# Tile 0 first in the last three pieces of a stage, a reordered norm, and GpSimd making three low parts

## The chip, the core and the metric

The kernel runs on one core of a Trainium2 chip. The metric is the device time of one execution in microseconds (us), the median of several runs. The engines are TensorE (PE, its weight loads are PEld), VectorE (DVE), ScalarE (ACT), GpSimd (POOL) and SyncE (SP), which here only issues weight transfers.

## The reference, cut to what matters

Two layers act on 256 rows of 1024 float32 values. Each layer has two sub-layers, and each sub-layer ends in a residual and two normalizations:

```python
shift, scale, gate = ada_modulation(c, w_mod_mix[layer], b_mod_mix[layer])
h = normalize(x) * (1.0 + scale) + shift
mix = token_mixer(h, pos, w_in[layer], ...)
x = layer_norm(DEEPNORM_ALPHA * x + (1.0 + gate) * mix, ln_mix_g[layer], ln_mix_b[layer])
shift, scale, gate = ada_modulation(c, w_mod_ffn[layer], b_mod_ffn[layer])
h = normalize(x) * (1.0 + scale) + shift
ff = swiglu(h, ...)          # layer 0; moe_swiglu(h, ...) with top 2 of 8 experts in layer 1
x = layer_norm(DEEPNORM_ALPHA * x + (1.0 + gate) * ff, ln_ffn_g[layer], ln_ffn_b[layer])
```

`token_mixer` is three branches (two kinds of attention and a pooling mixer), gated and merged, and ends in `merged @ w_out`. `swiglu` is `(silu(h @ w1) * (h @ w3)) @ w2`.

## The kernel before

**Pieces.** All weights stream through the core in pieces of 1 MB (128 x 2048 values). SyncE loads a piece into one of six slots of `w_raw`. ScalarE rounds it into `w_hi` (three slots; L467, in the experts L711), and VectorE makes the remainder `w_lo = w_raw - w_hi` (L830, L1219). A float32 product is then three matmuls: hi x hi, hi x lo and lo x hi (L1344 to L1346). Activations are split in the same way, into `actT_hi` (ScalarE, L501) and `actT_lo` (VectorE, L916). Pieces called "mod" carry the weights of the next sub-layer's shift, scale and gate. VectorE alone works on those (L855) and adds them up in `mod_acc`.

**Semaphores.** `split_hi` counts rounded pieces. `piece_used` counts pieces whose `w_raw` slot is free again, which is when `w_lo` is there. `split_used` counts pieces whose `w_hi` and `w_lo` slots TensorE has finished with. ScalarE rounds piece j only after TensorE has finished piece j - 3. The order of work on every engine is written out by hand; there is no planner.

**Tiles and stages.** The 256 rows are two tiles of 128. A piece is used on tile 0 and then on tile 1, 12 matmuls each. The stages are: MIX of layer 0 (27 pieces for TensorE: in, gate, branch, out), DENSE (33 pieces), MIX of layer 1, and a loop over eight experts. In MIX, piece "out" (n, h) is column half n and row half h of `w_out`, in the order (0,0), (1,0), (0,1), (1,1). DENSE goes by panels: A and B are up-projections, C is the down-projection. The gated panel is turned (transposed) by TensorE and split into `gT_hi` and `gT_lo` (L654, L1116) before its C pieces. The last panel is half as wide, so the last three pieces are C (4,0), C (4,1) and C (5,0).

**The end of a stage.** The last two pieces run tile by tile: both on tile 0, which signals `out_sent` (or `y_sent`), then both on tile 1 (L1612 to L1621, L1688 to L1695). In DENSE the last panel is turned after C (4,0) has run on both tiles (L1699). Then `open_sublayer` (L1370) broadcasts shift and scale over all rows by matmuls with ones (L1367, 4 float32 matmuls in 8 passes), transposes tile 0 of the new h (L1362), and broadcasts gate (L1378). `second_tile` transposes tile 1 (its `gate1_ready` wait is for ScalarE's L495). The next stage's first three pieces run on tile 0, then on tile 1; `second_tile` stands after piece 1 on tile 0. At the start of the experts there are no such pieces: the router follows tile 1.

**The norm between stages** (`norms`, L919 for VectorE, L504 for ScalarE, called three times, for `sub` 1, 2 and 3). For tile t VectorE does: `residual` (L892, L895), `statistics` of it (L875, L878 to L880), `inverse_std` (L884, after ScalarE's square root L484), `layer_norm` (L900, L901), `statistics` of x, `inverse_std`, `modulate` (L906, L909), `rest_of_h` (L916). L906 needs 1 + scale, which ScalarE makes in place (L489) after L1367. The order on VectorE is: `ahead(0)`, tile 0 up to the statistics of x, `ahead(1)`, residual and statistics of tile 1, modulation of tile 0, layer norm of tile 1, `rest_of_h` of tile 0, statistics and modulation of tile 1, `ahead(2)`, `rest_of_h` of tile 1. `ahead(i)` is the rounding (ScalarE) or the low part (VectorE) of the next stage's piece i.

**GpSimd** clears `mod_acc` (L416), and its queue issues the transfers of biases, norm rows and small tables (L418 to L437). It clears `yacc` and `zeros` before the experts (L451, L452). It does no arithmetic on weights.

Of the kernel before, what the change touches and what calls it, by code (L numbers as in the profile page):

```python
# [23 lines left out]
F32 = mybir.dt.float32  # L24
# [6 lines left out]
P = 128  # L31
# [168 lines left out]
def trunk(nc, I, consts, out):  # L200
    with ExitStack() as ctx:
# [70 lines left out]

        ident = cst[:, C_IDENT:C_IDENT + P]
# [26 lines left out]
        x_ready = sem("x_ready")  # L300
# [112 lines left out]
        def _(gp):  # L413
# [9 lines left out]

            nc.gpsimd.memset(mod_acc[:, :], 0.0).then_inc(acc_zero, 1)
# [4 lines left out]
            for layer in range(DEPTH):  # L429
# [4 lines left out]
                for par in range(2):  # L434
# [8 lines left out]
                        I["ln_mix_b"][bass.ds(layer, 1), :].rearrange("a d -> (a d)"))  # L443
                if layer < 1:
# [3 lines left out]
                    ln_rows(I["ln_ffn_g"][0], I["ln_ffn_b"][0])  # L448
                else:
# [9 lines left out]
        def _(act):  # L459
# [44 lines left out]
            def norms(sub, n, free, held, ahead):  # L504


                ahead(0)
                root(n + 1, 0)
                ahead(1)
                root(n + 2, 0)  # L510
                one_plus_scale(sub, free)
                root(n + 3, 1)
                ahead(2)
                round_h(sub, 0, held)
                root(n + 4, 1)
                one_plus_gate(sub, held)
                round_h(sub, 1, held)
# [13 lines left out]
            for layer in range(DEPTH):  # L531
# [111 lines left out]
                def panel_events(stretch, panels, split_base, panel0, blocks):  # L643
# [6 lines left out]
                    def gT_part(p):  # L650
                        act.wait_ge(gT_sent, panel0 + p + 1)
                        w = panels[p]
                        for b in range(blocks):
                            ins = A(gT_hi[:, b, 0:w // P, :], ps[:, HW1 + 2 * b, 0:w].rearrange("p (c q) -> p c q", q=P), ACT.Copy)  # L654
# [168 lines left out]
        def _(dve):  # L823
# [95 lines left out]
            def norms(chain, sub, n, free, held, f, f_done, n_ln, ahead):  # L919
# [3 lines left out]
                ahead(0)  # L923
# [21 lines left out]
                ahead(2)  # L945
# [25 lines left out]
            for layer in range(DEPTH):  # L971
# [119 lines left out]
                def yT_rest(c):  # L1091
# [4 lines left out]
                layer_loads = [MIX.landed[s] + DENSE.landed[s] for s in range(RING)]  # L1096
                stream(MIX, [layer * layer_loads[s] + MOD0.landed[s] for s in range(RING)], sbase,
# [3 lines left out]
                      layer * 64 + 32,  # L1101
                      lambda i: rest_of_piece(DENSE, i, sbase + MIX.n_split))
                assert chain.n == DVE_MIX_STEPS, chain.n

                def panel_events(stretch, panels, split_base, panel0, blocks):
# [6 lines left out]
                    def gT_part(p):  # L1112
                        dve.wait_ge(gT_hi_ready, panel0 + p + 1)
                        w = panels[p]
                        for b in range(blocks):
                            ins = TTn(gT_lo[:, b, 0:w // P, :], ps[:, HW1 + 2 * b, 0:w].rearrange("p (c q) -> p c q", q=P),  # L1116
                                      gT_hi[:, b, 0:w // P, :].bitcast(F32), ALU.subtract)
# [19 lines left out]
                if layer < 1:  # L1137
                    chain = Chain(dve, dve_ffn, 0)
                    stream(DENSE, [MOD0.landed[s] + MIX.landed[s] for s in range(RING)], MIX.n_split,
                           MOD0.n + MIX.n, 6 * MODS, 2, panel_events(DENSE, DENSE_PANELS, MIX.n_split, 0, 2))  # L1140
                    norms(chain, 2, 6, 4, 0, lambda t, c: bank(2 * t + c),
                          lambda t: dve.wait_ge(split_used, LAYER_SPLITS + SPLIT) if t else dve.wait_ge(y_sent, 1), 64,
                          lambda i: rest_of_piece(MIX, i, LAYER_SPLITS))
                    assert chain.n == DVE_DENSE_STEPS, chain.n
                else:
# [63 lines left out]
                    dve.wait_ge(yacc_zero, 1)  # L1209
                    with nc.Fori(0, EXPERTS, engines=[dve.engine], hint_back_edge=True, head_slot={dve.engine: 0}) as e:  # L1210
# [128 lines left out]
        def _(pe):  # L1339
# [30 lines left out]
            def open_sublayer(sub, free, held, gate_pieces=None):  # L1370
# [25 lines left out]
            for layer in range(DEPTH):  # L1396
# [147 lines left out]
                for i in range(SPLIT):  # L1544
# [4 lines left out]
                    if i == 1:  # L1549
# [6 lines left out]
                for i, piece in enumerate(MIX.pieces):  # L1556
# [41 lines left out]
                    elif h == 0:  # L1598
                        if n == 0:
                            pe.wait_ge(mT_hi_ready, layer * 2 + 1)  # L1600
                            pe.wait_ge(mT_lo_ready, layer * 2 + 1)
                        if n == 0:
# [294 lines left out]
```

## Time and profile before

| | |
|---|---|
| median of 3 runs | 1860.01 us (1859.79 to 1860.46) |
| the profiled execution | 1864.31 us |
| its span, first to last instruction | 1861.5 us |
| TensorE busy | 1686.1 us (91% of the span) |
| VectorE busy | 1408.1 us (76%) |
| ScalarE busy | 1035.7 us (56%) |
| GpSimd busy | 26.1 us (1%) |
| mean DMA rate | 270 GB/s |

A share of busy time is a mean over all stages. The chain that ended last says which engine's work or wait set the end at each moment. A timeline row gives start, duration, engine, source line, operation, output and inputs with shapes, how many instructions are merged, and in brackets how long the engine had been idle before and what released it. Matmul durations overlap in the pipeline, so the rate is read from the distance between starts.

### The profile page before, as it was taken

The page shows a single profiled execution, that of the slowest core. Times are in us where ns is not written, and L with a number is a line of the kernel's source. Part 1 is how long each engine was busy: PE and PEld are TensorE (multiplying, and loading weights), DVE is VectorE, ACT ScalarE, POOL GpSimd, SP SyncE. Part 2 cuts the span into 40 slices and gives each one's busy share as a digit, 9 for nine tenths or more (in the row PEclk, how much of TensorE's full clock was granted, in tenths as well). Part 3 has the DMA queues.
Part 4 walks back from the last instruction along what each step waited for, and adds up shares of the span by engine and source line. Part 5 has one row for each costly group of instructions (what it writes and reads, how often), then busy time and mean ns, then how long its engine had stood idle before and what let it go on. Part 6 is the DMA issues. An engine that isn't in the chain of part 4 may idle for free.

```text
span 1861.5 us, 21366 instructions
## 1 busy us (share of the span) xinstructions
PE 1686.1 (91%) x7620; PEld 1340.1 (72%) x7621; DVE 1408.1 (76%) x1201; ACT 1035.7 (56%) x822; POOL 26.1 (1%) x32
## 2 busy tenths in 40 slices
PE   1899979998999857999999989999999899999995
PEld 0687758886787736777877768888677677887773
DVE  7785877676876874897888865556589688788887
ACT  1465334433465424777767745545477577776772
POOL 0100000000100000000000000000000000000000
PEclk9898989999998977999999989999999899999998
DMA  9874458765574352998998975676499799899992
GB/s 366 312 275 159 138 201 293 272 249 171 195 271 156 113 203 102 375 381 304 367 345 303 391 275 181 215 229 212 157 377 382 254 371 387 306 366 337 331 393 81
DMA packets 210539, 502.36 MB, mean 270 GB/s; under 512 B 9138, under 2 KB 13410, under 8 KB 210482
## 3 DMA queue, kind: packets, MB, share of 16 engines
q1 hardware_dynamic: 208770, 496.15, 74.4%
q0 software_dynamic: 1712, 5.43, 0.9%
q8 instruction: 39, 0.64, 0.2%
q14 instruction: 18, 0.14, 0.0%
HBM read 500.50 MB, written 1.05 MB: 269 GB/s over the span
## 4 chain that ended last, share of the span: by engine, by line
PE 78%; DVE 14%; issue 6%; ACT 1%; DMA 1%; POOL 0%; DVEq 0%; SPq 0%; ACTq 0%; POOLq 0%
PE ps L1344 21%; PE ps L1346 21%; PE ps L1345 21%; DVE w_lo L1219 4%; PE ps L1350 3%; PE ps L1351 3%; PE ps L1738 2%; PE ps L1851 2%; DVE mod_acc L855 1%; DVE w_lo L830 1%; PE ps L1776 1%; DVE stats L875 1%; PE ps L1468 1%; DVE gates L1024 1%; DVE hbuf L906 1%
## 5 line engine op out<-in xcount | busy, mean ns | idle before, releaser
L1219 DVE TENSOR_TENSOR w_lo<-w_raw,w_hi 128x2048 fp32r<-128x2048 f32 x333 | 757.7, 2289 | 228.0 <-ACT w_hi L711 225.7
L711 ACT CAST w_hi<-w_raw 128x2048 fp32r<-128x2048 f32 x333 | 634.5, 1910 | 254.5 <-PE ps L1346 165.0
L1344 PE MATMUL ps<-w_hi,actT_hi 128*128 128x512 f32 (+1 forms) x1536 | 613.7, 400 | 41.0 <-DVE w_lo L1219 16.6
L1346 PE MATMUL ps<-w_hi,actT_lo 128*128 128x512 f32 (+1 forms) x1536 | 598.4, 390 | 0.0
L1345 PE MATMUL ps<-w_lo,actT_hi 128*128 128x512 f32 (+1 forms) x1536 | 597.8, 389 | 0.0
L1344 PEld LDWEIGHTS ps<-w_hi,actT_hi 128*128 128x128 f32 x1536 | 292.8, 191 | 117.3 <-issue 29.6
L1346 PEld LDWEIGHTS ps<-w_hi,actT_lo 128*128 128x128 f32 x1536 | 292.3, 190 | 60.9
L1345 PEld LDWEIGHTS ps<-w_lo,actT_hi 128*128 128x128 f32 x1536 | 293.2, 191 | 57.0 <-issue 1.7
L830 DVE TENSOR_TENSOR w_lo<-w_raw,w_hi 128x2048 fp32r<-128x2048 f32 x90 | 205.8, 2289 | 120.7 <-ACT w_hi L467 120.5
L467 ACT CAST w_hi<-w_raw 128x2048 fp32r<-128x2048 f32 x90 | 171.2, 1909 | 132.9 <-PE ps L1346 124.7
L1350 PE MATMUL ps<-w_hi,gT_hi 128*128 128x512 f32 x336 | 141.7, 422 | 14.8 <-DVE gT_hi L1246 14.8
L1351 PE MATMUL ps<-w_lo,gT_hi 128*128 128x512 f32 x336 | 137.9, 410 | 0.0
L855 DVE SCALAR_TENSOR_TENSOR mod_acc<-w_raw,c_act,mod_acc 128x512 f32<-128x512 f32 x192 | 130.5, 746 | 0.4 <-DMA w_raw<-in_w_mod_mix_dram 0.4
L1344 PE MATMUL ps<-w_hi,gT_hi 128*128 128x512 f32 x256 | 104.2, 407 | 7.6 <-DVE gT_lo L1242 3.8
L1345 PE MATMUL ps<-w_lo,gT_hi 128*128 128x512 f32 x256 | 103.5, 404 | 0.0
L1346 PE MATMUL ps<-w_hi,gT_lo 128*128 128x512 f32 x256 | 102.8, 401 | 0.0
L1350 PEld LDWEIGHTS ps<-w_hi,gT_hi 128*128 128x128 f32 x336 | 66.3, 197 | 42.9 <-DVE w_lo L1219 28.3
L1351 PEld LDWEIGHTS ps<-w_lo,gT_hi 128*128 128x128 f32 x336 | 66.4, 198 | 14.9
L1344 PEld LDWEIGHTS ps<-w_hi,gT_hi 128*128 128x128 f32 x256 | 49.3, 193 | 23.1 <-issue 7.3
L1346 PEld LDWEIGHTS ps<-w_hi,gT_lo 128*128 128x128 f32 x256 | 49.3, 192 | 11.9
L1345 PEld LDWEIGHTS ps<-w_lo,gT_hi 128*128 128x128 f32 x256 | 49.2, 192 | 11.2
L721 ACT ACTIVATE silu<-ps 128x512 f32<-128x512 f32 x56 | 33.6, 599 | 39.2 <-PE ps L1346 38.9
(238 smaller groups left out, 1174.5 us busy)
## 6 DMA issues: line engine op xcount, KB each, us to landing
w_raw<-in_exp_w_dram SPq DMA_DIRECT2D x336, 1024.0 KB, 6.8
w_raw<-in_ffn_w_dram SPq DMA_DIRECT2D x33, 1024.0 KB, 5.2
w_raw<-in_w_mod_mix_dram SPq DMA_DIRECT2D x24, 1024.0 KB, 9.0
w_raw<-in_w_mod_ffn_dram SPq DMA_DIRECT2D x24, 1024.0 KB, 6.0
w_raw<-in_w_gate_dram SPq DMA_DIRECT2D x24, 1024.0 KB, 6.5
w_raw<-in_w_in_dram SPq DMA_DIRECT2D x14, 1024.0 KB, 7.1
w_raw<-in_w_out_dram SPq DMA_DIRECT2D x8, 1024.0 KB, 5.1
w_raw<-in_w_branch_c_dram SPq DMA_DIRECT2D x4, 1024.0 KB, 5.2
```

The lines of the kernel that those rows point to most:

```text
L467: nc.scalar.copy(w_hi[:, j % SPLIT, :], w_raw[:, i % RING, :]).then_inc(split_hi, 1)
L711: nc.scalar.copy(w_hi[:, i % SPLIT, :], w_raw[:, i % RING, :]).then_inc(split_hi, 1)
L830: TTn(w_lo[:, j % SPLIT, :], w_raw[:, i % RING, :], w_hi[:, j % SPLIT, :].bitcast(F32), ALU.subtract).then_inc(piece_used, 1)
L855: ins = STT(acc, w[:, k, n * BANK:(n + 1) * BANK], c_act[:, 2 * (q % 4) + k:2 * (q % 4) + k + 1], acc, ALU.mult, ALU.add)
L1219: TTn(w_lo[:, i % SPLIT, :], w_raw[:, i % RING, :], w_hi[:, i % SPLIT, :].bitcast(F32), ALU.subtract).then_inc(piece_used, 1)
L1344: MM(to, hi, w_h, start=first, stop=False)
L1345: MM(to, hi, w_l, start=False, stop=False)
L1346: return MM(to, lo, w_h, start=False, stop=last)
L1350: MM(to, packed, w_h, start=first, stop=False)
L1351: return MM(to, packed, w_l, start=False, stop=last)
L1738: ins = MM(to, part[:, t, k * P:(k + 1) * P], pick[:, t, b * P:(b + 1) * P], start=t == 0, stop=t == 1)
L1851: ins = MM(bank(2 * t + c), place[:, b, t * P:(t + 1) * P], hbuf[:, b, c * BANK:(c + 1) * BANK], start=b == 0, stop=b == blocks - 1)
```

## The change

VectorE no longer makes the low parts of the next stage's first three pieces at the three seams. GpSimd does, in `rest_of_first`. `ahead` is gone from VectorE's `norms`, and VectorE waits on `piece_used` for the three before its next stream. At a stage's end the last three pieces run on tile 0 and then on tile 1. In DENSE the last panel is turned after C (4,0) on tile 0 only, and the last panel's `gT` has its own place, in `h_lo`. The norm modulates tile 0 before it touches tile 1. The broadcast of gate (`send_gate`) stands on its own: it waits for `rows_read`, which VectorE sets after tile 1's residual has been read, and it comes after piece 0 on tile 0; `second_tile` comes after piece 2 on tile 0. The first MIX stage of layer 0 keeps its order.

```diff
+        gT_end_hi, gT_end_lo = (h_lo[:, part, 0:BANK].rearrange("p (b c q) -> p b c q", b=2, q=P) for part in range(2))
+        def gT_parts(p, panels):
+            return (gT_end_hi, gT_end_lo) if p == len(panels) - 1 else (gT_hi, gT_lo)
...
# GpSimd
+            def rest_of_first(split_base):
+
+                for i in range(SPLIT):
+                    gp.wait_ge(split_hi, split_base + i + 1)
+                    nc.gpsimd.tensor_tensor(w_lo[:, i, :], w_raw[:, i, :], w_hi[:, i, :].bitcast(F32),
+                                            ALU.subtract).then_inc(piece_used, 1)
...
                 ln_rows(I["ln_mix_g"][bass.ds(layer, 1), :].rearrange("a d -> (a d)"),
                         I["ln_mix_b"][bass.ds(layer, 1), :].rearrange("a d -> (a d)"))
+                rest_of_first(layer * LAYER_SPLITS + MIX.n_split)
                 if layer < 1:
                     gp.wait_ge(gate_sent, 2)
                     fresh_acc(I["b_mod_mix"][1:2, :], 2)
                     gp.wait_ge(x_ready, 2)
                     ln_rows(I["ln_ffn_g"][0], I["ln_ffn_b"][0])
+                    rest_of_first(LAYER_SPLITS)
...
# ScalarE, norms
+                root(n + 1, 0)
                 ahead(0)
-                root(n + 1, 0)
-                ahead(1)
                 root(n + 2, 0)
                 one_plus_scale(sub, free)
+                round_h(sub, 0, held)
+                ahead(1)
                 root(n + 3, 1)
                 ahead(2)
-                round_h(sub, 0, held)
+                one_plus_gate(sub, held)
                 root(n + 4, 1)
-                one_plus_gate(sub, held)
                 round_h(sub, 1, held)
...
# VectorE, norms
-                ahead(0)
                 dve.wait_ge(gate1_ready, sub)
                 f_done(0)
                 residual(chain, f, 0)
...
                 statistics(chain, x, 0)
-                ahead(1)
-                f_done(1)
-                residual(chain, f, 1)
-                statistics(chain, hbuf, 1)
                 inverse_std(chain, n + 2, 0)
                 dve.wait_ge(scale_ready, sub + 1)
                 modulate(chain, 0, free)
+                f_done(1)
+                residual(chain, f, 1)
+                dve.sem_inc(rows_read, 1)
+                rest_of_h(sub, 0, held)
+                statistics(chain, hbuf, 1)
                 inverse_std(chain, n + 3, 1)
                 chain.step(layer_norm(chain, 1))
-                rest_of_h(sub, 0, held)
                 statistics(chain, x, 1)
                 inverse_std(chain, n + 4, 1)
                 modulate(chain, 1, free)
-                ahead(2)
                 rest_of_h(sub, 1, held)
                 dve.sem_inc(x_ready, 1)
...
+                if layer:
+                    dve.wait_ge(piece_used, LAYER_PIECES + MOD0.n + SPLIT + RING)
...
+                    dve.wait_ge(piece_used, first_split)
...
# TensorE
+            def send_gate(sub, held):
+
+                if sub:
+                    pe.wait_ge(rows_read, sub)
                 for q in range(2):
                     ins = MM(bank(held + 2 + q), ones, mod_acc[:, (4 + q) * BANK:(5 + q) * BANK], start=True, stop=True)
                 ins.then_inc(gate_sent, 1)
...
-                    if i == 1:
+                    if layer and i == 0:
+                        send_gate(2, 0)
+                    if i == (2 if layer else 1):
                         second_tile(layer * 2, 0)
...
+                        merged_T(1)
+                    elif (n, h) == (1, 0):
+                        project_out(j, n, h, 0)
+                    else:
+
                         if n == 0:
+                            pe.wait_ge(mT_hi_ready, layer * 2 + 2)
+                            pe.wait_ge(mT_lo_ready, layer * 2 + 2)
+                        ins = project_out(j, n, h, 0)
+                        if n == 1:
+                            ins.then_inc(out_sent, 1)
+                            for m, (n, h) in enumerate([(1, 0), (0, 1), (1, 1)]):
+                                project_out(j - 2 + m, n, h, 1).then_inc(split_used, 1)
...
-                            if b == 0 and i == 1:
-                                second_tile(1, 4)
+                            if b == 0 and i == 0:
+                                send_gate(1, 4)
+                        if b == 0:
+                            second_tile(1, 4)
...
+                            if j >= stretch.n_split - SPLIT:
+                                ins = down(j, p, h, 0)
+                                if j == stretch.n_split - SPLIT:
+                                    turn(p + 1)
+                                if j == stretch.n_split - 1:
+                                    ins.then_inc(y_sent, 1)
+                                    for m, (_, p, h) in enumerate(stretch.pieces[-SPLIT:]):
+                                        down(j - SPLIT + 1 + m, p, h, 1).then_inc(split_used, 1)
                                 continue
...
                 else:
+                    send_gate(3, 4)
                     second_tile(3, 4)
```

## Rows read from the trace of the kernel before

**Rows 1.** The page, chain that ended last, shares of the span.

```profile
PE 78%; DVE 14%; issue 6%; ACT 1%; DMA 1%; POOL 0%; DVEq 0%; SPq 0%; ACTq 0%; POOLq 0%
```

**Rows 2.** Timeline, TensorE, 247 to 300: start us, us, engine, line, shapes, [idle before].

```profile
247.45 3.59 PE L1367 MATMUL ps<-mod_acc,cst 128*128 128x512 f32 x8
...
260.38 1.97 PE L1362 MATMUL ps<-cst,hbuf 128*128 128x128 f32 x8 [9.33 <-DVE hbuf L909]
...
270.44 1.03 PE L1362 MATMUL ps<-cst,hbuf 128*128 128x128 f32 x8
...
272.22 0.50 PE L1344 MATMUL ps<-w_hi,actT_hi 128*128 128x512 f32 x1 [0.75 <-DVE w_lo L830]
...
299.32 0.39 PE L1346 MATMUL ps<-w_hi,actT_lo 128*128 128x512 f32 x1
```

**Rows 3.** Timeline, TensorE, 444 to 481.

```profile
444.48 0.47 PE L1344 MATMUL ps<-w_hi,gT_hi 128*128 128x512 f32 x1 [1.63 <-DVE gT_lo L1116]
...
455.75 3.60 PE L1367 MATMUL ps<-mod_acc,cst 128*128 128x512 f32 x8
468.52 1.97 PE L1362 MATMUL ps<-cst,hbuf 128*128 128x128 f32 x8 [9.18 <-DVE hbuf L909]
...
480.37 0.50 PE L1344 MATMUL ps<-w_hi,actT_hi 128*128 128x512 f32 x1 [0.70 <-DVE w_lo L830]
```

**Rows 4.** Timeline, TensorE, 663 to 692.

```profile
663.80 3.59 PE L1367 MATMUL ps<-mod_acc,cst 128*128 128x512 f32 x8
680.59 1.97 PE L1362 MATMUL ps<-cst,hbuf 128*128 128x128 f32 x8 [13.19 <-DVE hbuf L909]
...
689.66 1.94 PE L1362 MATMUL ps<-cst,hbuf 128*128 128x128 f32 x8 [4.51 <-DVE hbuf L909]
```

**Rows 5.** Timeline, VectorE, 242 to 269.

```profile
242.28 1.29 DVE L892 TENSOR_TENSOR hbuf<-ps,gate 128x512 f32<-128x512 f32 x2 [1.33 <-PE ps L1346]
...
244.93 1.28 DVE L875 BATCH_NORM_STATS2 stats<-hbuf 128x6 f32<-128x512 f32 x2
...
247.19 1.29 DVE L900 SCALAR_TENSOR_TENSOR hbuf<-hbuf,mv,lnrow 128x1024 f32<-128x1024 f32 x1
248.51 1.28 DVE L901 SCALAR_TENSOR_TENSOR x_sb<-hbuf,rstd,lnrow 128x1024 f32<-128x1024 f32 x1
...
251.39 0.15 DVE L880 TENSOR_SCALAR veps<-mv 128x1 f32<-128x1 f32 x1
...
258.13 1.40 DVE L906 SCALAR_TENSOR_TENSOR hbuf<-x_sb,mv,ps 128x512 f32<-128x512 f32 x2
...
266.49 0.15 DVE L880 TENSOR_SCALAR veps<-mv 128x1 f32<-128x1 f32 x1
...
267.11 1.41 DVE L906 SCALAR_TENSOR_TENSOR hbuf<-x_sb,mv,ps 128x512 f32<-128x512 f32 x2
```

**Rows 6.** Timeline, VectorE, 662 to 694.

```profile
662.49 1.28 DVE L892 TENSOR_TENSOR hbuf<-ps,gate 128x512 f32<-128x512 f32 x2
...
692.30 1.28 DVE L916 TENSOR_TENSOR actT_lo<-ps,actT_hi 128x512 fp32r<-128x512 f32 x2
```

**Rows 7.** Timeline, ScalarE, 251 to 263.

```profile
251.69 1.06 ACT L489 ACTIVATE ps<-ps 128x512 f32<-128x512 f32 x2
...
258.17 1.88 ACT L467 CAST w_hi<-w_raw 128x2048 fp32r<-128x2048 f32 x1
...
262.38 0.60 ACT L501 ACTIVATE actT_hi<-ps 128x512 fp32r<-128x512 f32 x1 [0.25 <-PE ps L1362]
```

**Rows 8.** Timelines of GpSimd and VectorE, 478 to 482 and at 692.

```profile
478.03 2.28 DVE L830 TENSOR_TENSOR w_lo<-w_raw,w_hi 128x2048 fp32r<-128x2048 f32 x1
...
478.76 2.69 POOL L416 MEMSET mod_acc<- 128x3072 f32 x1
...
692.37 1.80 POOL L451 MEMSET yacc<- 128x2048 f32 x1 [47.79 <-DVEq L947]
```

**Rows 9.** Windows, TensorE: window, length, busy (count), granted clock, DMA share, GB/s.

```profile
254.00:257.00 3.00, 0.00 (x0) 0.52 0.73 177
```

More of the change, by code:

```diff
@@ L299, in trunk @@
         h_ready, hT_sent, hT_hi_ready, hT_lo_ready = sem("h_ready"), sem("hT_sent"), sem("hT_hi_ready"), sem("hT_lo_ready")
-        x_ready = sem("x_ready")
+        x_ready, rows_read = sem("x_ready"), sem("rows_read")
         dve_start, dve_mix, dve_ffn, act_mix = sem("dve_start"), sem("dve_mix"), sem("dve_ffn"), sem("act_mix")
@@ L917, in rest_of_h, with norms @@
                         ALU.subtract).then_inc(hT_lo_ready, 1)
-            def norms(chain, sub, n, free, held, f, f_done, n_ln, ahead):
-                ahead(0)
+            def norms(chain, sub, n, free, held, f, f_done, n_ln):
                 dve.wait_ge(gate1_ready, sub)
@@ L1115, in gT_part @@
                         for b in range(blocks):
-                            ins = TTn(gT_lo[:, b, 0:w // P, :], ps[:, HW1 + 2 * b, 0:w].rearrange("p (c q) -> p c q", q=P),
-                                      gT_hi[:, b, 0:w // P, :].bitcast(F32), ALU.subtract)
+                            hi, lo = (part[:, b, 0:w // P, :] for part in gT_parts(p, panels))
+                            ins = TTn(lo, ps[:, HW1 + 2 * b, 0:w].rearrange("p (c q) -> p c q", q=P), hi.bitcast(F32), ALU.subtract)
                         ins.then_inc(gT_lo_ready, 1)
@@ L1597, in _ @@
                         ins.then_inc(split_used, 1)
[L1598 to L1602, printed above, removed]
-                            pe.wait_ge(branch_read, layer * 6 + 4)
+                    elif (n, h) == (0, 0):
+                        pe.wait_ge(mT_hi_ready, layer * 2 + 1)
+                        pe.wait_ge(mT_lo_ready, layer * 2 + 1)
+                        pe.wait_ge(branch_read, layer * 6 + 4)
                         for t in range(TT):
@@ L1685, in swiglu @@
                                 pe.wait_ge(gT_lo_ready, panel0 + p + 1)
-                            if j == stretch.n_split - 2:
-                                continue
-                            if j == stretch.n_split - 1:
-                                for b in range(blocks):
-                                    ins = down(j - 1, p - 1, 1, b)
-                                    if b == blocks - 1:
-                                        ins.then_inc(split_used, 1)
-                                    ins = down(j, p, h, b)
-                                    ins.then_inc(split_used if b == blocks - 1 else y_sent, 1)
+                            if j >= stretch.n_split - SPLIT:
[6 more added lines that the diff above has]
+                                        down(j - SPLIT + 1 + m, p, h, 1).then_inc(split_used, 1)
                                 continue
```

28 lines of the change are left out of this document (9 added, 19 removed).

## The prediction

> **What bounds the kernel now.** I read first the page's chain that ended last: TensorE holds 78% of it and VectorE 14% [rows 1]. So time comes only from what TensorE waits for, and the change touches three places, the seams between stages, where it waits for VectorE. I call them seam 1 (attention part to dense part, layer 0), seam 2 (dense part to layer 1) and seam 3 (attention part to the experts). TensorE's timeline of each comes next. At seam 1 the eight passes that broadcast scale and shift (L1367) end at 251.04, then TensorE is idle 9.33 us until tile 0's transposes at 260.38, and the wait is for VectorE's L909 [rows 2]. Seam 2 has 9.18 us, and 1.63 us before it for the last gT_lo [rows 3]. Seam 3 has 13.19 us for tile 0 and 4.51 us for tile 1 [rows 4]. VectorE's timeline shows what it does meanwhile, a serial norm [rows 5]. I measure seams 1 and 2 by when TensorE starts tile 1 of the next stage's first three pieces. One piece on one tile is 12 matmuls; from 272.22 to 299.32 there are 119 steps, so 0.2277 us each and 2.73 us a piece [rows 2]. Piece 2 of tile 0 starts at 272.22 and 480.37; with 2.79 for its slower first step, tile 1 starts at 275.0 and 483.15 now.
>
> **Earlier start of tile 0's norm.** Three pieces instead of two are left for tile 1, so tile 0's sum is ready one piece, 2.73 us, sooner: VectorE's L892, now at 242.28, can start near 239.4. At seam 3 it now starts at 662.49, behind the w_lo subtraction that the norm issues first, ahead(0) [rows 6]; the last three pieces of tile 1 end at 663.80, so afterwards it starts at 663.80 - 3 x 2.73 = 655.6, 6.9 us sooner. Tile 1's pieces give their weight slots back later than now, which costs nothing: cast 0 goes behind the first square root, at 243.9 at seam 1, and GpSimd is through with piece 0 at about 251, before tile 0 needs it.
>
> **What is late next.** From L892 to the second L880 are 9.11 us, and L880 to L906 takes 0.62 when nothing is in between (266.49 to 267.11) [rows 5]: the norm of tile 0 could reach L906 9.73 after it starts, at 249.1, 455.4 and 665.3 (at seam 2 tile 0's sum will be ready at 445.7, which is 457.7 below less 3.6 for L1367 and 3 x 2.8 for tile 1's pieces). But L906 needs 1+scale, and that comes after all of tile 1's matmuls: L1367 ends at 251.04, 457.7 (459.35 less the 1.63 us wait, which goes because tile 0 of two other pieces covers the last turn) and 667.39 [rows 2 to 4]. ScalarE adds 1.06 us [rows 7] and two hand-overs make it 1.2. So L906 starts at M = 252.2, 458.9 and 668.6. Some 3 us of the earlier start are thus lost at each seam. Tile 0's transposes follow at M + 2.25 (258.13 to 260.38) [rows 2, 5].
>
> **After M, on VectorE:** modulation 2.89, residual of tile 1 2.65 (242.28 to 244.93), first half of L916 0.65 [rows 5, 6]. TensorE starts piece 0 at M + 6.25 and is done with it at M + 9; the two gate broadcasts (about 1.8 at full clock, 8 passes being 3.59) end at M + 10.8. VectorE goes on with the rest of L916 and the first statistics of tile 1 and reaches L900 at M + 9.25.
>
> **GpSimd.** ScalarE's second L501 ends 2.60 after the transposes begin, the cast is 1.88 [rows 7]: GpSimd starts piece 1 at M + 6.75. No row has a GpSimd subtraction. Its memset of 2048 elements, one write stream, takes 1.80 [rows 8]; that is the lower end, and three streams (two reads, one write) one after another, 5.4, the upper. VectorE needs 2.28 for it [rows 8]. I take 4.5, two and a half streams, as the two reads are the part least likely to overlap. The Trainium skill ("GPSIMD Engine Reference", section 3.1) measures 4497 ns for a two-input operation of 2048 elements against 2293 on VectorE; the VectorE figure agrees with the row, the other is shown by no run here.
>
> **Do GpSimd and VectorE meet?** In the one overlap that rows show, GpSimd's memset at 478.76 inside L830 (two SBUF inputs), L830 keeps its 2.28 [rows 8]; but that GpSimd instruction only writes. The new one reads two SBUF tiles while VectorE runs L900 and L901, which read two SBUF tiles each. The price of that meeting is from 0 to the rest of the GpSimd instruction per VectorE instruction. I take the upper end for the one wait that is certain to be met, and VectorE keeping its turn afterwards, since it follows its own instruction within 0.03 us (L900 end to L901) [rows 5]. The Trainium skill ("SBUF — State Buffer", section "Who interferes with whom") has this as a rule: a VectorE instruction with two SBUF inputs contends with a GpSimd instruction that reads SBUF, the later one blocks for the whole of the other, and a memset does not count. The memset row agrees with its last part; the rest is against this change, and without it my sum would be that of the first rival.
>
> **The sum.** Piece 1 of GpSimd runs from M + 6.75 to M + 11.25. L900 waits 2.0 for it and ends at 12.55, L901 at 13.9. GpSimd's piece 2 (cast ready at M + 10.9) runs from 13.9 to 18.4. TensorE does piece 2 of tile 0 until 21.15; tile 1's transposes, ready at 9.25 + 2.0 + 4.20 + 0.62 + 2.25 = 18.35, follow it, and tile 1's first matmul comes 2.0 after they start (half of the transposes' 1.03, cast 0.60, half of L916's 1.28, hand-overs) [rows 2, 6, 7], at M + 23.15.
> Seam 1: 275.35 against 275.0, a loss of 0.35. Seam 2: 482.05 against 483.15, a gain of 1.1. Seam 3 has no matmuls in between: transposes of tile 1 at 668.6 + 18.35 = 686.95 against 689.66, and L916 behind them no longer waits for the L830 just before 692.30 (it would have started 1.9 after the transposes, not 2.64; 0.65 counting its second half) [rows 4, 6], a gain of 3.35. What comes after each seam is TensorE-bound at the old rhythm, so all of it is kept. Together 4.1. The profiled execution took 1864.31 around its span of 1861.5, the median is 1860.01: 1864.31 - 4.1 = 1860.2 there, and 1855.9 against the median; I write 1856.
>
> The rest costs nothing: ln rows, the memset of mod_acc and its bias are issued by GpSimd behind the subtractions, up to 9 us later than now, but the first use is L855 some 20 us behind the seam; yacc is zeroed after tile 1's norm as now; the gate broadcast has moved behind piece 0, where TensorE would wait for w_lo anyway, and the wait added before it (rows_read, set at M + 5.5) is over by then; VectorE's added wait for GpSimd's three pieces stands before its stream, whose first work (piece 3) needs a cast that comes after tile 1's piece 0. If those covers failed, the price would be the memset's 2.69 [rows 8] each.
>
> **Clock.** [...] Piece 0 and the gates have 1.75 us of slack before piece 2 becomes possible even in the fastest case, so I price it at 0, with 1 us a seam as the other end.
>
> **Rivals.**
> (a) The engines don't meet: L900 at M + 9.25, GpSimd's piece 2 from 11.25 to 15.75, tile 1 starts at M + 20.5, seam 3's transposes at M + 16.4. Gains 2.3, 3.75 and 5.3, together 11.35: 1848.7. For it: the memset row. Against: that was a write alone.
> (b) The other side: GpSimd's piece 2 gets in between L900 and L901. It waits at that moment in either case, since its cast is done at M + 10.9. L900 ends at 12.55, GpSimd runs to 17.1, L901 to 18.4, tile 1's transposes at 23.0, its matmuls at 25.0. Losses 2.2, 0.75 and 1.3, together 4.25: 1864.3. It decides as soon as L901 is handed out after GpSimd's waiting instruction. At a subtraction of 5.4 the loss is about 9: 1869.
> (c) The subtraction is slow, VectorE keeps its turn: each us of it moves seams 1 and 2 by two and seam 3 by one, so 5.4 us takes 4.5 and leaves nothing: 1860. At 3.6 it gives 4.5 more: 1851.4.
>
> **Chances.** Forecast and its near sizes (c at under 5.2 us) 0.37, (a) 0.27, (b) 0.18, (c) slow or the clock eating the gain 0.18. A run of this kernel tells 0.2%, 3.7 us, from no change. Faster: (a) 0.27 and most of the forecast's own cases, 0.29, since its 4.1 is just past the line, so 0.56. Same: 0.25, from the forecast, (c) and the mild end of (b). Slower: 0.19. The range goes from 1846 (a with a subtraction of 3.9) to 1866 (b).
>
> **What would show it.** Right: tile 0's L892 starts 2.7 us before the end of one more piece, L906 starts 1.2 after L1367's end and VectorE stands idle some 3 us before it; at each seam the GpSimd rows are near 4.5 us; L900 of tile 1 either starts late or takes up to 2 us longer. Wrong: L900 at M + 9.3 and 1.29 long (a); over 4 us between L900's and L901's ends (b); a subtraction far from 4.5; a wait in TensorE for w_lo of piece 1.

## The result, and the profile after

The change makes the kernel slower: 1865.59 us (median of 15 runs, 1859.18 to 1869.68) against 1858.58 of the kernel before (15 runs, 1853.97 to 1860.61), ratio 1.0033, 95% interval 1.0024 to 1.0043. That is a loss of 6.1 us (4.5 to 8.0). The forecast was 1856.0, a gain of 4.1; the other side, rival (b), was 1864.3. The time lies inside the stated range, at its far end, and went the other way than the forecast.

The profiled executions themselves stand the other way round: span 1860.4 after, 1861.5 before. A ledger of both shows why. Each row counts ScalarE's casts of weight pieces (w_hi<-w_raw, 423 in either kernel), so the same work lies between two of them; cast 26 is the last before seam 1, casts 27 to 29 are the next stage's first three pieces, cast 30 is the first one of tile 1's rhythm, and so on at the others.

```
stretch (cast to cast)                    before   after   before - after, us
start to 26                                232.1   229.7    +2.4
26 to 30    seam 1                          45.9    50.1    -4.2
30 to 59                                   158.9   158.9     0.0
59 to 63    seam 2                          49.3    50.4    -1.0
63 to 86                                   162.2   163.8    -1.6
86 to 100   seam 3                         105.1   105.5    -0.4
100 to 422  loop over the experts         1074.5  1068.6    +5.9
```

The differences are taken before rounding. The seams cost 5.6 us, which lies in what the ratio says. The change does not touch the work of the other rows. The loop over the experts is the same in all ten kernels of this document and takes from 1067.9 to 1074.5 us in their profiled executions; that of before is the longest, with the granted clock low for 47.8 us of it, against 30.7 in after. The start to cast 26 takes from 228.9 to 232.1, again with before as the longest. So the seams are read from the traces and the whole from the ratio.

First the chain that ended last, on the page after, answering [rows 1]. It says nothing: one step more of TensorE and one less of VectorE.

```profile
PE 79%; DVE 13%; issue 6%; ACT 1%; DMA 0%; POOL 0%; DVEq 0%; SPq 0%; ACTq 0%; POOLq 0%
```

VectorE's timeline at seam 1, after (start, duration, engine, line, shapes, idle before it). L907, L915, L916 and L921 are L892, L900, L901 and L906 of [rows 5].

```profile
237.09 1.29 DVE L907 TENSOR_TENSOR hbuf<-ps,gate 128x512 f32<-128x512 f32 x2 [3.18 <-PE ps L1362]
...
242.00 1.29 DVE L915 SCALAR_TENSOR_TENSOR hbuf<-hbuf,mv,lnrow 128x1024 f32<-128x1024 f32 x1
243.32 1.29 DVE L916 SCALAR_TENSOR_TENSOR x_sb<-hbuf,rstd,lnrow 128x1024 f32<-128x1024 f32 x1
...
249.79 1.41 DVE L921 SCALAR_TENSOR_TENSOR hbuf<-x_sb,mv,ps 128x512 f32<-128x512 f32 x2 [3.00 <-ACT ps L504]
...
258.69 3.40 DVE L915 SCALAR_TENSOR_TENSOR hbuf<-hbuf,mv,lnrow 128x1024 f32<-128x1024 f32 x1
262.12 5.49 DVE L916 SCALAR_TENSOR_TENSOR x_sb<-hbuf,rstd,lnrow 128x1024 f32<-128x1024 f32 x1
```

The same two instructions take 1.29 us each for tile 0 and 3.40 and 5.49 for tile 1. No idle time is shown before them: the wait for the other engine stands inside the duration, as busy time. GpSimd's timeline of the same stretch:

```profile
243.59 5.40 POOL L434 TENSOR_TENSOR w_lo<-w_raw,w_hi 128x2048 fp32r<-128x2048 f32 x1 [17.76 <-ACT w_hi L482]
256.43 10.10 POOL L434 TENSOR_TENSOR w_lo<-w_raw,w_hi 128x2048 fp32r<-128x2048 f32 x2 [7.44 <-ACT w_hi L482]
```

The subtraction of piece 0 begins inside tile 0's L916, which ends at 244.61, and lasts from there 4.4 us. Pieces 1 and 2 stand in one row. Alone the subtraction takes 4.52 (the least of its nine), so piece 1 ends near 261.0, and L915, begun at 258.69, ends 1.1 later, at 262.09. L916 starts 0.03 us after that, but piece 2 has waited since 261.0 and goes first: 262.09 + 4.5 is 266.6, where the GpSimd row ends (266.53), and L916 ends 1.1 later. Seams 2 and 3 show the same pair:

```profile
469.34 2.90 DVE L915 SCALAR_TENSOR_TENSOR hbuf<-hbuf,mv,lnrow 128x1024 f32<-128x1024 f32 x1
472.28 5.49 DVE L916 SCALAR_TENSOR_TENSOR x_sb<-hbuf,rstd,lnrow 128x1024 f32<-128x1024 f32 x1
```
```profile
681.84 3.23 DVE L915 SCALAR_TENSOR_TENSOR hbuf<-hbuf,mv,lnrow 128x1024 f32<-128x1024 f32 x1
685.10 5.40 DVE L916 SCALAR_TENSOR_TENSOR x_sb<-hbuf,rstd,lnrow 128x1024 f32<-128x1024 f32 x1
```

TensorE's timeline at seam 1, after, to be set beside [rows 2] (L1383, L1378 and L1360 are L1367, L1362 and L1344 of before; L1400 is the gate broadcast):

```profile
244.98 3.59 PE L1383 MATMUL ps<-mod_acc,cst 128*128 128x512 f32 x8
...
252.03 1.90 PE L1378 MATMUL ps<-cst,hbuf 128*128 128x128 f32 x8 [3.46 <-DVE hbuf L924]
256.10 0.76 PE L1360 MATMUL ps<-w_hi,actT_hi 128*128 128x512 f32 x1 [2.17 <-issue]
...
260.27 1.88 PE L1400 MATMUL ps<-mod_acc,cst 128*128 128x512 f32 x4
...
266.58 0.50 PE L1360 MATMUL ps<-w_hi,actT_hi 128*128 128x512 f32 x1 [1.67 <-POOL w_lo L434]
...
272.17 1.68 PE L1378 MATMUL ps<-cst,hbuf 128*128 128x128 f32 x8 [2.58 <-DVE hbuf L924]
274.30 0.76 PE L1360 MATMUL ps<-w_hi,actT_hi 128*128 128x512 f32 x1 [0.44 <-issue]
274.86 0.63 PE L1361 MATMUL ps<-w_lo,actT_hi 128*128 128x512 f32 x1
...
279.52 0.40 PE L1360 MATMUL ps<-w_hi,actT_hi 128*128 128x512 f32 x1
```

The 9.33 us ahead of tile 0's transposes are down to 3.46, but 2.17, 1.67 and 2.58 have come behind them. Tile 1's first piece, the twelve matmuls from 274.30 to 279.52, takes 5.22 us instead of the 2.73 that [rows 2] give. The windows of TensorE (window, length, busy and count, granted clock, DMA share, GB/s) say why: the clock is at 0.50, the lower of its two levels, 1.2 GHz, and 1.00 a few us later.

```profile
273.00:279.00 6.00, 5.56 (x15) 0.50 0.47 154
280.00:286.00 6.00, 6.00 (x28) 1.00 0.12 16
```

At seam 3 the transposes of tile 1 come at 695.06, and TensorE has waited 12.86 us for them:

```profile
695.06 1.94 PE L1378 MATMUL ps<-cst,hbuf 128*128 128x128 f32 x8 [12.86 <-DVE hbuf L924]
```

### The profile page after: what moved, and what is told of

Same layout as the page of the kernel before. It is cut to its first block, busy times and chain, and to the rows that moved or that the text cites. A ratio compares the mean times of both kernels' runs of the same rounds, so it can differ in the third digit from the quotient of the medians.

```text
span 1860.4 us, 21368 instructions
## 1 busy us (share of the span) xinstructions
PE 1684.5 (91%) x7620; PEld 1336.5 (72%) x7621; DVE 1406.9 (76%) x1192; ACT 1036.1 (56%) x822; POOL 72.4 (4%) x41
## 4 chain that ended last, share of the span: by engine, by line
PE 79%; DVE 13%; issue 6%; ACT 1%; DMA 0%; POOL 0%; DVEq 0%; SPq 0%; ACTq 0%; POOLq 0%
PE ps L1360 22%; PE ps L1362 21%; PE ps L1361 21%; DVE w_lo L1235 4%; PE ps L1366 3%; PE ps L1367 3%; PE ps L1761 2%; PE ps L1874 2%; DVE mod_acc L870 1%; PE ps L1799 1%; DVE x_sb L916 1%; PE ps L1383 1%; PE ps L1490 1%; DVE gates L1037 1%; DVE hbuf L915 1%
## 5 line engine op out<-in xcount | busy, mean ns | idle before, releaser
L1235 DVE TENSOR_TENSOR w_lo<-w_raw,w_hi 128x2048 fp32r<-128x2048 f32 x333 | 757.5, 2289 | 222.4 <-ACT w_hi L726 220.1
L1360 PE MATMUL ps<-w_hi,actT_hi 128*128 128x512 f32 (+1 forms) x1536 | 616.5, 401 | 49.3 <-issue 18.5
L1362 PE MATMUL ps<-w_hi,actT_lo 128*128 128x512 f32 (+1 forms) x1536 | 600.3, 391 | 0.0
L1360 PEld LDWEIGHTS ps<-w_hi,actT_hi 128*128 128x128 f32 x1536 | 294.5, 192 | 127.2 <-issue 35.7
L1362 PEld LDWEIGHTS ps<-w_hi,actT_lo 128*128 128x128 f32 x1536 | 293.3, 191 | 61.4
L845 DVE TENSOR_TENSOR w_lo<-w_raw,w_hi 128x2048 fp32r<-128x2048 f32 x81 | 185.2, 2288 | 109.2 <-ACT w_hi L482 109.0
L1366 PE MATMUL ps<-w_hi,gT_hi 128*128 128x512 f32 x336 | 140.8, 419 | 14.7 <-DVE gT_hi L1262 14.7
L1367 PE MATMUL ps<-w_lo,gT_hi 128*128 128x512 f32 x336 | 137.1, 408 | 0.0
L1360 PE MATMUL ps<-w_hi,gT_hi 128*128 128x512 f32 x248 | 99.8, 403 | 6.0 <-DVE gT_lo L1258 3.8
L1361 PE MATMUL ps<-w_lo,gT_hi 128*128 128x512 f32 x248 | 98.9, 399 | 0.0
L1362 PE MATMUL ps<-w_hi,gT_lo 128*128 128x512 f32 x248 | 98.5, 397 | 0.0
L1367 PEld LDWEIGHTS ps<-w_lo,gT_hi 128*128 128x128 f32 x336 | 65.8, 196 | 14.8
L1360 PEld LDWEIGHTS ps<-w_hi,gT_hi 128*128 128x128 f32 x248 | 46.9, 189 | 20.6 <-issue 5.5
L434 POOL TENSOR_TENSOR w_lo<-w_raw,w_hi 128x2048 fp32r<-128x2048 f32 x9 | 46.4, 5168 | 235.5 <-ACT w_hi L482 235.5
L1362 PEld LDWEIGHTS ps<-w_hi,gT_lo 128*128 128x128 f32 x248 | 46.9, 189 | 11.2
```

The source lines that it names most:

```text
L434: nc.gpsimd.tensor_tensor(w_lo[:, i, :], w_raw[:, i, :], w_hi[:, i, :].bitcast(F32), ALU.subtract).then_inc(piece_used, 1)
L845: TTn(w_lo[:, j % SPLIT, :], w_raw[:, i % RING, :], w_hi[:, j % SPLIT, :].bitcast(F32), ALU.subtract).then_inc(piece_used, 1)
L1235: TTn(w_lo[:, i % SPLIT, :], w_raw[:, i % RING, :], w_hi[:, i % SPLIT, :].bitcast(F32), ALU.subtract).then_inc(piece_used, 1)
L1360: MM(to, hi, w_h, start=first, stop=False)
L1361: MM(to, hi, w_l, start=False, stop=False)
L1362: return MM(to, lo, w_h, start=False, stop=last)
```

## The experiments

Two theories are set against each other in the first five runs. Theory A: a GpSimd instruction that reads SBUF and a VectorE instruction with two SBUF inputs exclude each other for a whole instruction, and that costs the change its gain. Theory B: the new order (1+scale behind tile 1's matmuls, the split pieces), or GpSimd's length alone. Each seam length below is cast to cast, as in the ledger. Lines that shift by the edits carry other numbers in each kernel; the operands tell which instruction it is.

```
kernel             seam 1  seam 2  seam 3   us sooner than before in all   ratio to before, 95% interval
before               45.9    49.3   105.1     -
after                50.1    50.4   105.5    -5.6     1.0033  1.0024-1.0043
e1 writes only       43.7    45.1    98.7   +12.8     0.9933  0.9915-0.9951
e2 on VectorE        45.7    47.4   102.6    +4.7     0.9978  0.9965-0.9990
e3 casts early       44.3    46.0    99.5   +10.6     0.9943  0.9925-0.9960
e4 held back         48.9    50.7   101.2    -0.5     0.9998  0.9989-1.0008
e7 GpSimd alone      46.9    51.9   106.5    -4.9     1.0024  1.0013-1.0036
e5 copy, one time    43.0    45.3    99.1   +13.0     -
e6 modulation 1st    46.6    46.1    98.3    +9.4     0.9925  0.9910-0.9941
e8 root first        41.4    42.7    97.8   +18.4     0.9916  0.9899-0.9934
```

**e1: the same length, no reads.** From the kernel after; it leaves the low parts of these three pieces at zero.

```diff
-  nc.gpsimd.tensor_tensor(w_lo[:, i, :], w_raw[:, i, :], w_hi[:, i, :].bitcast(F32), ALU.subtract).then_inc(piece_used, 1)
+  for part in (yacc[:, :, :], yacc[:, 0, :]):
...
+      nc.gpsimd.memset(part, 0.0).then_inc(filled, 1)
+  nc.gpsimd.memset(w_lo[:, i, :].bitcast(F32), 0.0).then_inc(piece_used, 1)
```

> The changed kernel with GpSimd's nine subtractions replaced by three memsets each (1.8 + 0.9 + 1.8 us and two short hand-overs, about 4.9 us, so as long as a subtraction alone or a little longer), which only write: w_lo of the first three pieces of a stage is zero, so the output is less exact. Theory A (GpSimd reading SBUF and VectorE's instructions with two SBUF inputs exclude each other, and that is the loss): L915 and L916 of tile 1 take 1.29 us again instead of 3.4 and 5.5; tile 1's transposes come 6.3 us earlier at seam 3 and 5 to 6 us earlier at seams 1 and 2, limited there by the memsets' length; total 1847 to 1852, 0.4 to 0.6% under the kernel before. Theory B (the new order, or the length of GpSimd's work as such, costs the time): L915 and L916 may get short, but the total stays at 1862 to 1867.

Measured 1844.69 us (before 1858.24), ratio 0.9933, 2.3 us under theory A's range and far from B's. GpSimd was as busy as with the subtraction, 4.6 us a piece, and VectorE did not notice:

```profile
257.52 2.81 POOL L440 MEMSET yacc<- 128x2048 f32 x2 [8.15 <-ACT w_hi L489]
260.28 1.82 POOL L441 MEMSET w_lo<- 128x2048 f32 x1
```
```profile
259.93 1.28 DVE L922 SCALAR_TENSOR_TENSOR hbuf<-hbuf,mv,lnrow 128x1024 f32<-128x1024 f32 x1
261.25 1.28 DVE L923 SCALAR_TENSOR_TENSOR x_sb<-hbuf,rstd,lnrow 128x1024 f32<-128x1024 f32 x1
```

These are GpSimd's and VectorE's timelines at seam 1 of e1; the memsets run on through both VectorE instructions. The new order with a GpSimd that only writes gains 12.8 us at the seams, near rival (a)'s 11.35, and is 18.4 us shorter there than the kernel after. So the order is good, and the length of GpSimd's work is not the cost: its reads are. The Trainium skill ("SBUF — State Buffer", section "Who interferes with whom") has just these conditions, two SBUF inputs on VectorE against a GpSimd read, with writes exempt; the traces of after and e1 agree.

**e2: the new order, low parts back on VectorE.**

```diff
# GpSimd, rest_of_first
-                    nc.gpsimd.tensor_tensor(...)
# VectorE, norms (ahead(i) is rest_of_piece of piece i)
                 inverse_std(chain, n + 2, 0)
+                ahead(0)
                 dve.wait_ge(scale_ready, sub + 1)
...
                 rest_of_h(sub, 0, held)
+                ahead(1)
...
                 chain.step(layer_norm(chain, 1))
+                ahead(2)
```

> The changed kernel with the three low parts given back to VectorE: piece 0 in its 3 us of waiting for 1+scale, piece 1 after tile 0's L931, piece 2 after tile 1's L916. All else, ScalarE's order too, stays changed. Theory A: no contention, but 4.6 us more on VectorE's path after 1+scale; seams 1, 2, 3 end 0.1 us later, 1.3 earlier, 0.8 earlier than in the kernel before: 1856 to 1859, 0.0 to 0.15% under it. Theory B, in the form that the order itself costs the time: 1862 or more, as in the changed kernel.

Measured 1854.79, ratio 0.9978: at the seams 4.7 us better than before, and 1.2 us under the range expected. VectorE's timeline at seam 1 of e2:

```profile
247.38 2.29 DVE L844 TENSOR_TENSOR w_lo<-w_raw,w_hi 128x2048 fp32r<-128x2048 f32 x1
250.28 1.41 DVE L920 SCALAR_TENSOR_TENSOR hbuf<-x_sb,mv,ps 128x512 f32<-128x512 f32 x2 [0.60 <-ACT ps L503]
```

The new order pays even without GpSimd, since piece 0 fits into VectorE's wait for 1+scale, which shrinks from 3.00 to 0.60. Against e1 it lacks 8.1 us at the seams. VectorE does two pieces there in its serial norm, 4.6 us a seam, and a part of that is hidden.

**e3: GpSimd keeps reading, but out of the way.** All casts go ahead of 1+scale; piece 2's subtraction waits for rows_read, so that it follows tile 1's residual.

```diff
# GpSimd, rest_of_first
+                    if i == 2:
+                        gp.wait_ge(rows_read, sub)
...
# ScalarE, norms
   root(n + 1, 0)
   ahead(0)
+  ahead(1)
   root(n + 2, 0)
+  ahead(2)
   one_plus_scale(sub, free)
   round_h(sub, 0, held)
-  ahead(1)
   root(n + 3, 1)
-  ahead(2)
```

> The changed kernel with the meeting taken away by time: ScalarE rounds all three pieces before 1+scale is there (it is idle then), so GpSimd makes pieces 0 and 1 while VectorE runs one-input instructions or waits, and GpSimd holds piece 2 until tile 1's residual is done (rows_read). Theory A: GpSimd at about 244.6 to 253.6 (seam 1), then from M + 5.4 to M + 9.9 (M the start of tile 0's L921), L915 waits 0.7 us at most, L916 not at all; tile 1 starts on the next stage at M + 19 instead of about M + 24.5; total 1845 to 1849, 0.5 to 0.7% under the kernel before. Theory B: GpSimd's subtractions are as long, the order is the same: at best 1860.

Measured 1845.82, ratio 0.9943, inside theory A's range. GpSimd's and VectorE's timelines at seam 1 of e3:

```profile
245.68 9.91 POOL L436 TENSOR_TENSOR w_lo<-w_raw,w_hi 128x2048 fp32r<-128x2048 f32 x2 [17.83 <-ACT w_hi L484]
257.46 4.55 POOL L436 TENSOR_TENSOR w_lo<-w_raw,w_hi 128x2048 fp32r<-128x2048 f32 x1 [1.87 <-DVEq L953]
```
```profile
260.79 2.31 DVE L917 SCALAR_TENSOR_TENSOR hbuf<-hbuf,mv,lnrow 128x1024 f32<-128x1024 f32 x1
263.13 1.28 DVE L918 SCALAR_TENSOR_TENSOR x_sb<-hbuf,rstd,lnrow 128x1024 f32<-128x1024 f32 x1
```

No subtraction is left for GpSimd when L917 ends, and L918 keeps its 1.28. L917 takes 1.0 more than its 1.29, about until the subtraction ends (262.01); 0.7 at most was expected. Tile 1 starts at M + 21.1 (273.00 less L923's 251.88), not at M + 19: piece 0 of tile 0 took 5.26 us at the low clock (258.19 to 263.45) instead of 2.73, which the expectation left out.

**e4: one more wait.** GpSimd's pieces 1 and 2 wait until tile 1's layer norm (L917, L918) is done.

```diff
   for i in range(SPLIT):
       gp.wait_ge(split_hi, split_base + i + 1)
+      if i:
+          gp.wait_ge(normed, sub)
```

> The changed kernel with one wait added: GpSimd starts pieces 1 and 2 only when tile 1's layer norm (L915, L916) is done. Theory A: both take 1.29 us, tile 1's h is there 6.3 us sooner, but piece 2's low part comes at M + 21 and tile 1 starts at about M + 25.7 at seams 1 and 2 (about 1 us later than in the changed kernel), while seam 3 gains 6.3 us: total 1858 to 1861. Theory B (what counts is when GpSimd is done): GpSimd ends 4 us later than in the changed kernel at each seam, so every seam is later and the total is 1870 or more.

Measured 1856.69, ratio 0.9998: a wait added to the kernel after takes some 6 us off it (0.35%, from the two ratios). That is 1.3 us under theory A's range and far from B's. Against the kernel after, seams 1 and 3 are 1.2 and 4.3 us shorter (1 longer and 6.3 shorter were expected). L917 and L918 of tile 1 are 1.29 and 1.28, and GpSimd's two pieces run at 262.44 for 9.05 us, 4.5 each, undisturbed. What is late now is TensorE, idle for 3.86 before piece 1, waiting for GpSimd:

```profile
267.10 0.77 PE L1363 MATMUL ps<-w_hi,actT_hi 128*128 128x512 f32 x1 [3.86 <-POOL w_lo L436]
```

**e7: GpSimd alone.** From the kernel before, in the old order, with only the three subtractions moved to GpSimd.

```diff
# VectorE, norms
-                ahead(0)
...
-                ahead(1)
...
-                ahead(2)
# GpSimd, at each of the three seams
+                rest_of_first(...)
```

> The kernel before with one part of the change alone: GpSimd makes the three low parts, the order of pieces and norm is the old one. Theory A: GpSimd's pieces 1 and 2 meet tile 1's L895 (1.5 us) and L900 (3 us and more), and in the old order tile 0's low part of h waits behind L900 and L901; each seam is 2 to 4 us later than in the kernel before, total 1864 to 1872. Theory B (the new order is what costs, GpSimd's help is good): VectorE is rid of 4.6 us at each seam and TensorE starts each next stage about 2 to 4 us sooner, 1848 to 1855.

Measured 1863.55 (before 1859.17), ratio 1.0024: just under A's range, far from B's. Taking 3 x 2.28 us of work a seam off VectorE, for which TensorE waits there, makes the kernel slower by 0.24% (0.13 to 0.36). VectorE's timeline at seam 1 of e7:

```profile
250.94 2.53 DVE L905 SCALAR_TENSOR_TENSOR hbuf<-x_sb,hbuf 128x512 f32<-128x512 f32 x2
...
258.29 4.64 DVE L910 SCALAR_TENSOR_TENSOR hbuf<-hbuf,mv,lnrow 128x1024 f32<-128x1024 f32 x1
262.96 1.28 DVE L911 SCALAR_TENSOR_TENSOR x_sb<-hbuf,rstd,lnrow 128x1024 f32<-128x1024 f32 x1
```

L905, the residual, also reads two SBUF tiles and waits 1.2; L910 waits 3.4, behind the subtraction of piece 2 that began at 257.33, 0.96 before it. So the exclusion is no matter of the new order.

**e5: a GpSimd copy in place of the subtraction.** One read and one write; the low parts hold w_hi instead of the remainder.

```diff
-  nc.gpsimd.tensor_tensor(w_lo[:, i, :], w_raw[:, i, :], w_hi[:, i, :].bitcast(F32), ALU.subtract).then_inc(piece_used, 1)
+  nc.gpsimd.tensor_copy(w_lo[:, i, :], w_hi[:, i, :].bitcast(F32)).then_inc(piece_used, 1)
```

> The changed kernel with GpSimd's two-input subtraction replaced by a copy of w_hi into w_lo, a GpSimd instruction with one SBUF input and the same output; the low parts of nine pieces are wrong, so the output is not the reference's, and only the seams are read, not the total. If any GpSimd read excludes VectorE's second input, L915 and L916 of tile 1 are longer than 1.29 us by what is left of the copy (1.8 to 2.5 us long); if only a two-input GpSimd instruction does, they take 1.29 us.

It ran once, 1841.95 us. GpSimd's and VectorE's timelines at seam 1 of e5:

```profile
256.77 1.90 POOL L434 CAST w_lo<-w_hi 128x2048 fp32r<-128x2048 f32 x1 [9.93 <-ACT w_hi L481]
260.80 2.74 POOL L434 CAST w_lo<-w_hi 128x2048 fp32r<-128x2048 f32 x1 [2.14 <-ACT w_hi L481]
```
```profile
260.50 1.28 DVE L915 SCALAR_TENSOR_TENSOR x_sb<-hbuf,rstd,lnrow 128x1024 f32<-128x1024 f32 x1
```

The copy that begins inside L915 takes 0.84 more than the other, and L915 ends 0.98 after the copy's start. Six of the nine copies start so, and all six take 2.73 to 2.80; the other three take 1.89 or 1.90. A single read is enough, then, and the wait goes in this direction too. No copy was running when a two-input VectorE instruction started, so the case that the expectation was about did not occur, and VectorE waiting for a copy is not shown.

**e6: modulation first.** In the kernel after 1+scale comes behind tile 1's three pieces and costs VectorE 3.0 us of waiting. Here TensorE broadcasts shift and scale ahead of those pieces, and GpSimd's piece 1 is held until tile 1's residual is read (as piece 2 in e3) and its piece 2 until tile 1's layer norm is done (as in e4).

```diff
# TensorE, MIX: between tile 0's and tile 1's last three pieces (DENSE: send_modulation(4))
                             ins.then_inc(out_sent, 1)
+                            send_modulation(0)
...
# TensorE, open_sublayer
-                send_modulation(free)
+                if sub == 0:
+                    send_modulation(free)
...
# ScalarE, norms
                 root(n + 1, 0)
+                one_plus_scale(sub, free)
                 ahead(0)
                 root(n + 2, 0)
-                one_plus_scale(sub, free)
+                ahead(1)
                 round_h(sub, 0, held)
-                ahead(1)
+                ahead(2)
                 root(n + 3, 1)
-                ahead(2)
...
# GpSimd, rest_of_first
+                    if i == 1:
+                        gp.wait_ge(rows_read, sub)
+                    if i == 2:
+                        gp.wait_ge(normed, sub)
```

The gate broadcast and tile 1's transposes move too, behind piece 1 on tile 0.

> The forecast named the broadcast of shift and scale behind tile 1's pieces as what is late next. Here it stands between the last piece of tile 0 and the three of tile 1 (at all three seams), so that 1+scale is ready before tile 0's norm needs it; ScalarE makes it first and its casts follow; GpSimd makes piece 0 at once, piece 1 after rows_read and piece 2 after tile 1's layer norm, outside VectorE's instructions with two SBUF inputs; the gate broadcast and tile 1's transposes stand after piece 1. Theory A (the seam is VectorE's chain from tile 0's sum on): L921 starts 9.8 us after L907 instead of 12.7, TensorE's idle of 3.45 us before tile 0's transposes shrinks to under 1 us, the granted clock stays at full there and piece 0 takes 2.73 us instead of 4.3 to 5.5; total 1833 to 1840, 1.0 to 1.4% under the kernel before. Rival (the seam ends by TensorE's and GpSimd's work after the norm, the start of the modulation is hidden anyway): as the kernel with early casts, 1845 to 1848.

Measured 1845.25 (before 1859.17), ratio 0.9925: faster, but 5 us short of theory A's range, and where the rival's range (1845 to 1848) begins. Two steps came as expected: tile 0's L925 begins 9.73 after its L911 (246.01 less 236.28), and TensorE is idle for 0.48 before tile 0's transposes instead of 3.46. The clock did not stay at full: it fell at 251.2, in TensorE's next idle stretch, and piece 0 of tile 0 took 5.26 us (252.33 to 257.59).

```profile
252.33 0.77 PE L1365 MATMUL ps<-w_hi,actT_hi 128*128 128x512 f32 x1 [2.76 <-issue]
```

ScalarE's timeline at seam 1 shows what took most of it back:

```profile
262.49 1.09 ACT L514 ACTIVATE gate<-ps 128x512 f32<-128x512 f32 x2 [7.80 <-PE ps L1406]
263.46 0.21 ACT L503 ACTIVATE std<-veps 128x1 f32<-128x1 f32 x1
```

Tile 1's last square root, whose input is ready at 260.42, is queued behind 1+gate, which waits for TensorE.

**e8: the root ahead of 1+gate.**

```diff
-  one_plus_gate(sub, held)
   root(n + 4, 1)
+  one_plus_gate(sub, held)
```

> As e6_modfirst, but ScalarE takes tile 1's last square root ahead of 1+gate, which waits for TensorE's gate broadcasts. In e6_modfirst that root was ready at 260.42 (VectorE's end of variance+eps) and started at 263.46, behind the gate's 1.09 us, which itself had waited for TensorE until 262.49. Theory A (at seam 1 and 2 the queue order on ScalarE was what set tile 1's modulation, and the clock nothing): tile 1's modulation starts at about 260.9 instead of 263.90; its transposes then wait only for the bank that 1+gate reads, free at 263.6, and start some 3 us sooner at seam 1 and 2 at seam 2, and up to 3 at seam 3 if the same order held there: seams by ScalarE's casts near 43.6 / 44 / 96-98, the time 1838 to 1841 (e6_modfirst 1845.25). Rival B (the rest of what e6_modfirst lacked is TensorE's low clock after its first, short idle stretch; the root hid beside it): within 1 us of e6_modfirst, 1844 to 1846, with TensorE still late with tile 0's pieces when tile 1's modulation is done.

Measured 1839.60 (before 1855.83), ratio 0.9916, inside theory A's range. The root now runs 0.03 us behind its input, and tile 1's transposes wait 1.18 instead of 3.78. ScalarE's and TensorE's timelines at seam 1 of e8:

```profile
261.55 0.20 ACT L503 ACTIVATE std<-veps 128x1 f32<-128x1 f32 x1 [5.76 <-DVE veps L899]
263.63 1.09 ACT L514 ACTIVATE gate<-ps 128x512 f32<-128x512 f32 x2 [1.87 <-PE ps L1406]
```
```profile
264.76 1.09 PE L1383 MATMUL ps<-cst,hbuf 128*128 128x128 f32 x8 [1.18 <-ACT gate L514]
```

Seam 1 is 5.1 us shorter than in e6 (3.0 were expected; a second low stretch of the clock, 6.8 us from 264.9 in e6, is gone too), seam 2 3.4, seam 3 0.5. Of that the ratio shows little, 0.9916 against 0.9925, with intervals that overlap: the profiled execution of e6 (1847.19) was 1.9 above its median, and the two kernels ran on different chips, beside runs of the kernel before that differ by 3 us themselves (1859.17 and 1855.83). So the trace shows theory A of that run, while the size of its gain in the whole is open. e8 beats the kernel before by 0.84% and, from the two ratios, the kernel after by 1.2%.

## Why the prediction was wrong, point by point

- **Tile 0's norm and M: right.** L907 to L921 takes 12.70 us, 12.8 were worked out; L921 starts 1.22 after L1383 ends (1.2); VectorE stands idle before it for 3.00, 3.23 and 3.00 at the three seams.
- **The subtraction: right.** 4.52 us alone, 4.5 taken. The Trainium skill's figure ("GPSIMD Engine Reference", section 3.1), 4497 ns, agrees with it.
- **The first wait: right.** L915 took 3.40, 2.90 and 3.23, 1.6 to 2.1 more than its 1.29; 2.0 was taken.
- **VectorE keeping its turn: this step failed.** L916 did not follow L915 in 0.03 us of work: it was handed over then, and waited 4.2, 4.2 and 4.1 for piece 2 in front of it. That is rival (b) as it was written, and its mechanism: an instruction that already waits goes before one that is only now handed out. The prediction had said that the point from which (b) decides is when L901 is handed out after GpSimd's waiting instruction. Its own times had the cast of piece 2 ready at M + 10.9, GpSimd free for it at 11.25 and L901's turn at 12.55, so the condition was met on paper, as the text of (b) says itself; the short hand-over was taken for a claim on the next turn, which it isn't. Between (b) and the forecast lie 8.35 us.
- **What is late after it: somewhat less than in (b).** Tile 1 starts at M + 24.5 and M + 24.0 at seams 1 and 2 (25.0), its transposes at M + 22.1 at seam 3 (23.0): 2.4 us in all.
- **The clock, priced at 0: mis-sized.** The fall beside tile 0's transposes stayed hidden, as argued: TensorE waits for GpSimd's piece 2 all the same. But the clock fell once more at seams 1 and 2, where tile 1 begins (272.6 and 484.3). Tile 1's first twelve matmuls take 5.22 and 4.33 us instead of 2.73: 2.5 and 1.6 us. The other end, 1 us a seam, was too low as well. The extra fall goes with the idle stretches of 1.67 and 2.58 us that (b) makes; in e3, where tile 1's transposes follow tile 0's pieces without a gap, tile 1 starts at full speed (0.47 for its first matmul). That the idle stretches are the cause was not tested by itself. Added up, the loss is 4.25 - 2.4 + 4.1 = 6.0, against 5.6 in the ledger and 6.1 (4.5 to 8.0) by the ratio. That (b)'s 4.25 comes this near is in part luck: two errors of it nearly cancel.
- **What was costed at nothing: right** as far as it shows. The ledger has 0.0 between seams 1 and 2. It has 1.6 between 2 and 3, where e7, with the same subtractions on GpSimd, is level with before (162.3 and 162.2), and where e6 and e8, with the same work in this stretch, take 161.0 and 163.7. So I take it for the difference of two executions, untested.
- **Rival (a)** would have been right for another instruction: e1 is that case, +12.8 at the seams against 11.35.

## What to carry to other kernels

Before moving elementwise work from VectorE to GpSimd, list for both the instructions' inputs in SBUF, not only their durations: in these runs GpSimd's subtraction and VectorE's two-input instructions took turns, a whole instruction each, and an engine's queue position gives no right to the next turn. In a profile such waits are no idle time but long durations: compare a line's mean with its least. If the work must go there, hold it with a semaphore until the other engine's two-input instructions are past, or let it begin well before them (e3 and e8 do some of both, at 0.57% and 0.84% under the kernel before). Holding alone can only move the wait: in e4 TensorE then waits for GpSimd.

## What the runs showed of the hardware that had not been expected

The cost of these turns is seen in two rows that group VectorE's layer norm by line (busy us, mean ns of one), in the kernel after; in the kernel before, both lines are at 10.3, 1285:

```profile
L916 DVE SCALAR_TENSOR_TENSOR x_sb<-hbuf,rstd,lnrow 128x1024 f32<-128x1024 f32 x8 | 22.8, 2850 | 0.3
L915 DVE SCALAR_TENSOR_TENSOR hbuf<-hbuf,mv,lnrow 128x1024 f32<-128x1024 f32 x8 | 16.0, 1994 | 0.3
```

- When VectorE issues two such instructions 0.03 us apart and GpSimd's next one already waits, GpSimd gets in between, at three seams of three.
- VectorE's instructions with one input in SBUF, or with one in SBUF and one in PSUM, ran at full speed beside a GpSimd subtraction: L890 at 244.64 kept its 1.28 beside the subtraction of 243.59, and in e6 L935 at 251.53 its 1.29 for two beside the one of 251.59.
- GpSimd's copy of 2048 elements takes 1.90 us, near its memset's 1.80, and its subtraction 4.52, 2.6 more. Whether the second read or the arithmetic makes that, no run separates.
